# Five activation tiles of a two-block transformer kernel, placed 64 bytes further along each partition

## What is computed

```python
x = x + 0.5 * swiglu(rmsnorm(x, ff1_norm), w_gate, w_up, w_down)
h = rmsnorm(x, mix_norm); proj = h @ w_in            # gmlp inputs, q, k, v, gates
y_a = gmlp_spatial_gating(gelu(a_in), ...)
y_b = stick_breaking_attention(q, k, v)              # 16 heads of 64
x = x + (g_a * (y_a @ w_branch_a) + g_b * (y_b @ w_branch_b)) @ w_out
x = x + 0.5 * swiglu(rmsnorm(x, ff2_norm), ...)
x = rmsnorm(x, final_norm)
# second block, layer 0 moba attention, layer 1 forgetting attention
h = h + merge_heads(attention(split_heads(q), split_heads(k), split_heads(v))) @ w_o
h = h + jnp.square(relu(rms_norm(h, mlp_norm) @ w_up)) @ w_down
```

## Time and profile before

| | |
|---|---|
| median of 3 runs | 1236.98 us (1236.93 to 1237.11) |
| the profiled execution | 1236.78 us, of which the span from first to last instruction is 1235.0 us |
| TensorE, matmuls | 1222.5 us busy (99%), 6847 |
| TensorE, weight loads | 1048.1 us (85%), beside the matmuls |
| vector engine | 835.0 us (68%) |
| scalar engine | 627.7 us (51%) |
| GpSimd | 82.9 us (7%) |
| HBM read | 219.52 MB, 179 GB/s over the span |
| granted TensorE clock | 1.000 as the mean of the span |

### The profile page before, as it was taken

The page is one execution under the profiler, slowest core; times in us unless marked ns, Lnnn a source line. Parts: engine busy times, 40 slices in busy tenths (PEclk is TensorE's granted clock), DMA queues, the critical chain, the costliest instruction groups (busy, mean ns, idle before and its releaser), DMA issues.

```text
span 1235.0 us, 17596 instructions
## 1 busy us (share of the span) xinstructions
PE 1222.5 (99%) x6847; PEld 1048.1 (85%) x6847; DVE 835.0 (68%) x1277; ACT 627.7 (51%) x965; POOL 82.9 (7%) x181
## 2 busy tenths in 40 slices
PE   8999999999999999999999999999999999999998
PEld 7888888898888888888888988888888888888886
DVE  6877766454675668777775766875656676876764
ACT  6544446565553446444455656544446455744443
POOL 0000000121000000000003210000000540000000
PEclk9999999999999999999999999999999999999999
DMA  7755666534855555655665445866653655676640
GB/s 237 238 184 186 204 193 194 183 115 115 294 173 169 170 155 175 214 179 186 194 195 169 123 136 188 261 195 191 189 171 105 173 155 166 198 246 189 191 148 35
DMA packets 174923, 221.74 MB, mean 180 GB/s; under 512 B 9100, under 2 KB 103912, under 8 KB 174840
## 3 DMA queue, kind: packets, MB, share of 16 engines
q1 hardware_dynamic: 173496, 216.86, 56.0%
q0 software_dynamic: 912, 2.71, 0.8%
q10 hardware_dynamic: 432, 1.05, 0.2%
HBM read 219.52 MB, written 1.06 MB: 179 GB/s over the span
## 4 chain that ended last, share of the span: by engine, by line
PE 95%; DVE 3%; ACT 1%; DMA 0%; issue 0%; ACTq 0%; DVEq 0%; POOLq 0%
PE bank L1414 55%; PE bank L1500 22%; PE bank L1507 11%; PE bank L1437 1%; PE bank L1671 1%; DVE w_lo L936 1%; PE bank L1654 1%; DVE xt L971 1%; PE bank L1644 1%; PE bank L1631 1%; PE bank L1629 1%; DVE x L1051 0%; PE bank L1675 0%; ACT xt L633 0%; DMA gain_rows<-in_ff_norm 0%; PE bank L1622 0%
## 5 line engine op out<-in xcount | busy, mean ns | idle before, releaser
L936 DVE TENSOR_TENSOR w_lo<-raw,w_hi 128x1024 fp32r<-128x1024 f32 (+1 forms) x448 | 491.4, 1119 | 199.8 <-ACT w_hi L595 199.5
L595 ACT ACTIVATE w_hi<-raw 128x1024 fp32r<-128x1024 f32 (+1 forms) x448 | 422.6, 972 | 277.9 <-PE bank L1507 141.7
L1500 PE MATMUL bank<-xt,w_hi 128*128 128x512 f32 x1216 | 317.0, 393 | 0.0
L1500 PEld LDWEIGHTS bank<-xt,w_hi 128*128 128x128 f32 x1216 | 216.3, 189 | 34.6
L1507 PEld LDWEIGHTS bank<-xt,w_lo 128*128 128x128 f32 x1216 | 170.6, 190 | 15.3
L1507 PE MATMUL bank<-xt,w_lo 128*128 128x256 f32 x1216 | 175.1, 282 | 0.0
L1414 PE MATMUL bank<-w_hi,xt 128*128 128x512 f32 x512 | 159.8, 393 | 0.9 <-DVE xq_lo L971 0.5
L1414 PE MATMUL bank<-w_hi,yt_lo 128*128 128x512 f32 x336 | 132.2, 394 | 0.0
L1414 PE MATMUL bank<-w_hi,yt_hi 128*128 128x512 f32 x336 | 130.9, 390 | 0.0
L1414 PE MATMUL bank<-w_lo,yt_hi 128*128 128x512 f32 x336 | 130.9, 390 | 0.0
L1414 PE MATMUL bank<-xt,w_hi 128*128 128x256 f32 x640 | 116.0, 283 | 0.0
(11 more groups left out here) (197 smaller groups left out, 1149.1 us busy)
## 6 DMA issues: line engine op xcount, KB each, us to landing
raw<-in_w_up SPq DMA_DIRECT2D x64, 512.0 KB, 4.2
raw<-in_w_down SPq DMA_DIRECT2D x64, 512.0 KB, 4.5
raw<-in_w_in SPq DMA_DIRECT2D x56, 512.0 KB, 4.6
raw<-in_ff_w_gate SPq DMA_DIRECT2D x88, 256.0 KB, 3.5
raw<-in_ff_w_up SPq DMA_DIRECT2D x88, 256.0 KB, 4.4
raw<-in_ff_w_down SPq DMA_DIRECT2D x88, 256.0 KB, 4.6
raw<-in_moba_w_qkv SPq DMA_DIRECT2D x24, 512.0 KB, 4.1
raw<-in_w_o SPq DMA_DIRECT2D x16, 512.0 KB, 3.8
```

The lines of the kernel that those rows point to most:

```text
L595: act.activation(w_hi[:, c % RING, 0:w], raw[:, c % RAW, 0:w], ACT.Copy).then_inc(s["hi_ready"], 1)
L936: dve.tensor_tensor(w_lo[:, c % RING, 0:w], raw[:, c % RAW, 0:w], w_hi[:, c % RING, 0:w].bitcast(F32), ALU.subtract).then_inc(s["lo_ready" ...
L1500: ins = pe.matmul(up_banks(m)[q][:], w_h[:, k % 2, q * P:(q + 1) * P], flat(xt[:, k, :, :]), start=k == 0, stop=False, skip_group_check=True)
```

## The change

A tile of 64 bytes is put in front of `xt` and another of 64 bytes behind `ht_lo`. Nothing reads or writes them. Between them stand `xt`, `yt_hi`, `yt_lo`, `ht_hi` and `ht_lo`, each 64 bytes further along the partition than before; all that follows stands 128 bytes further.

```diff
         side = sb("side", [P, TOK, D])
+        gap_in = sb("gap_in", [P, 16])
         xt = sb("xt", [P, KT, 2, S], F32R)
         xt_hi, xt_lo = xt[:, :, 0, :], xt[:, :, 1, :]
         yt_hi = sb("yt_hi", [P, KT, S], F32R)
         yt_lo = sb("yt_lo", [P, KT, S], F32R)
         ht_hi = sb("ht_hi", [P, 4, S], F32R)
         ht_lo = sb("ht_lo", [P, 4, S], F32R)
+        gap_out = sb("gap_out", [P, 16])
         work = [sb(f"work{n}", [P, 2, 512]) for n in range(3)]
```

## The result

The changed kernel takes 1245.04 us (median of 6 runs, 1244.62 to 1246.13), the kernel before beside it 1237.05 us: a ratio of 1.0064 with a 95% interval of 1.0054 to 1.0074. It is 8 us slower. The forecast was 1230.5 us with a range up to 1243.

The account below looks back on a forecast made before the run. TensorE's stream of matmuls was taken to bound the kernel. Gains of 4.2 + 0.5 us in projections and 1.8 in line 1507, 0 for 512-column matmuls, made 6.5 us off 1236.98: 1230.5 us, range 1220 to 1243.

Parts of the forecast that it names:

- the two terms together: 256-column matmuls on `xt`: projections of the attention stages win 4.2 + 0.5 us, line 1507 wins 1.8 us.
- No change: Whole kernel: independent reads or another cause for `xq`'s pace leave 1237.0 us; chance 0.17, including small losses eating the gain.
- the independence of the two reads: TensorE: loading the next weights takes no SBUF read bandwidth from the running matmul, so the sum would be zero.
- The sentence quoted beside it: Skill page on SBUF: "PE and ACT never wait on anyone", taken as also giving 1237.0 us.
- the third term of the sum: 3664 512-column matmuls of lines 1500 and 1414, activation moving or stationary: taken at 0, with 3.5 us as possible win.
- The third rival: Slower: 512-column matmuls stay disturbed, 4.7 ns each over 3664, giving 1247.7 us; chance 0.19, about half above 1243.
- modulo 128: Tile places in each partition counted modulo 128 bytes: the five moved tiles stand 64 off the weights, as `xq` already did.
- The trial that the prediction saw inside the profile: Attention projections before the change: `xq`, counted as 64 off, moves at 113.2 ns a matmul against 120.0 for `xt`.
- the forecast for the moving operand: 256-column matmuls with `xt` moving get faster: projection pairs at 5.65 to 5.8 us instead of 5.94, line 1507 runs shorter.

## Why the prediction was wrong

**Right.** What bounds the kernel: all of the 8 us is in the distances between the starts of matmuls. That the place of the two operands against each other sets a pace, and that the rows of `xq` show it: the 256-column matmuls gained 3.2 us in line 1507 (1.8 forecast, ends 1.8 and 7.5) and 3.2 us in the projections (4.7 forecast, ends 2.0 and 6.5). Line 1507 did better, with 69 of its 114 runs of 8 at 113 ns, and the projections worse, since only 14 of the 40 settled at 113 ns. That the two terms together gave 6.4 us where 6.5 were forecast is luck: one was 1.4 too low and the other 1.5 too high. *No change* fell, with 1245.0 us against the 1237.0 that it gave. So did the independence of the two reads, by the 5.8 ns above. The sentence quoted beside it from the Trainium skill, page "SBUF — State Buffer", section "Who interferes with whom", can also be read as one on waits for other engines, which no run here tests.

**Wrong: the third term of the sum.** "I take 0, the settled pace, because both `xt` at equal remainder and `xq` at 64 do find a free pace." Taken from 256-column matmuls with the activation moving, this was carried over to 512-column ones with the activation stationary, of which the trace had no row off distance 0. The premise behind it, that operands which stand alike disturb each other and an offset frees them, turned out the other way round in this role: with `yt` or `ht` as stationary, distance 0 is the best of all those measured (228.0 ns, against 229.9 to 234.5). At 64 they do not settle: in a `down` of the changed kernel the starts are 231, 229, 236, 231, 235, 231, 236 ns apart and so on to the last of the 24, where before they came down to 226 and 227 within the first few. That is 12.7 us for the 2448 with an activation as stationary. Line 1500, the other part of the term, kept its mean (+0.5 us), though no longer by settling: it now goes round through 226, 229 and 232.

The third rival named this mechanism, with 4.7 ns as the price, and was too low in its chance. Its measured price is 5.5 ns for `yt` and `ht` and 4.6 for `xt`, but on two thirds of the 3664 matmuls: 12.7 us where it had 17.2, which is most of the way from its 1247.7 to 1245.0. The row that it leaned on, the first matmul on `xq` with 281 ns, is of distance 192, where `yt` and `ht` lose only 1.9 ns; it is no measure of the loss at 64. The range held only half of this case, by my own count, and ended 2 us below the result.

**Wrong: "modulo 128".** The prediction counts places modulo 128 and has no row that shows this period. Modulo 256, `xq` stands at 192 before the change, not at 64, and 192 is the one good place for a moving 256-column operand. The change put `xt` at 64 and, through the 128 bytes behind `ht_lo`, moved `xq` from 192 to 64 as well: runs of `xq` at 113 ns went from 5 of 8 to 2 of 8. Its own distance isn't shown to be the reason: with `xq` left at 192 and `xt` at 64, 1 of 8 reaches it, and with both at 192 all 8 do. The trial that the prediction saw inside the profile was one of another distance. With `xt` alone at 192 the forecast for the moving operand comes true in full (114.5 ns, pairs at 5.64 us).

**A term that rests on less than I said.** That `xt` runs in 276 ns beside a load of 16 columns was read as proof that a smaller load doesn't disturb. At distance 64 a load of 16 columns cost nearly as much as one of 128, so the row shows no more than that this tile, at this distance, was free.

**Open.** Why 192 is good for a moving activation and 64 only now and then, why 0 alone is free for a stationary one, and why 96 loaded columns disturb less than 64. The runs give the paces by distance, not the order of the reads behind them. Whether the period comes from the memory's layout or from how far ahead TensorE reads was not tried.

## What to carry to other kernels

In this kernel, bound by a dense stream of matmuls in fp32r, the byte distance between the stationary and the moving tile modulo 256 was worth 0.5% in one direction and 1.2% in the other, for nothing but unused bytes between tiles. In another kernel bound in the same way it is worth a trial. Measure the distance between starts for each form of matmul and each distance: the busy time of the whole engine adds up gains and losses, and mean durations are not what a matmul costs. Price every role a tile has: the same shift won on `xt` as the moving operand and lost on it as the stationary one. And when a gap is put before one tile, everything behind it moves too: fill up to a whole number of 256 bytes behind it, or the comparison is of something else.

## What the runs showed of the hardware that was not expected

- Where the stationary operand lies changes the pace of a moving stream of 512 columns by 5.8 ns (227.8 against 233.6 with only the place of the stationary tile changed), while its load lasts 188 ns in both. A settled stream of 256 columns runs at 120.0 with the operands at distance 0 and at 113.2 at 192.
- The period is 256 bytes: with all five tiles moved, 0 and 256 give the same time (ratio 1.0), 64 costs 0.6%, 128 costs 1.2%, 192 wins 0.2%.
- Shifting everything by 64 bytes changes nothing (0.9999).
- Paces fall into short repeating patterns that hold for the length of a run (226, 229, 232 or 231, 236), and one form at one distance falls into different ones: the projections of the changed kernel come in pairs of 5.64 and 5.85 us by turns. That what ran before decides which one was not tried by itself.
- The cost at distance 64 is not in proportion to the columns loaded: 231.6, 231.7, 231.1, 228.7 and 233.3 ns for 16, 32, 64, 96 and 128.
